# Expert stage: the dots begin once the first head's experts are known, and the searches of heads 1 and 2 stand between them

## The chip, the cores and the metric

One Trainium2 chip, one of its NeuronCores. The metric is the device time of one execution in microseconds (us). Engines are named as in the profile: PE is TensorE, DVE is VectorE, ACT is ScalarE, POOL is GpSimd, SP is the sync engine. 1 MB tiles of weights are issued by SP (DMA queue q1), the gathers of experts by POOL (queue q0). Both queues are served by the same 16 DMA engines.

## The reference, cut to what matters

The program is two blocks on 256 tokens of width 1024. The second block has two layers, and each layer ends in `peer_ffn`, a layer of retrieved experts:

```python
q = (zb @ wq).reshape(128, Hp, 2, half)              # 8 heads, two halves of 128
s = jnp.einsum('thpd,hpnd->thpn', q, subkeys)        # 128 scores a half
s_top, i_top = lax.top_k(s, 16)
cand = s_top[:, :, 0, :, None] + s_top[:, :, 1, None, :]   # 16 x 16 sums
score, flat = lax.top_k(cand.reshape(128, Hp, 256), 16)
expert = i1 * 128 + i2                               # from i_top and flat
gate = jax.nn.softmax(score, axis=-1)
h = jnp.einsum('thkd,td->thk', u_tab[expert], zb)
act = gate * jax.nn.gelu(h, approximate=False)
return jnp.einsum('thk,thkd->td', act, v_tab[expert])
```

Each token has 8 heads of 16 experts, so 128 experts, and each expert is a row of `u` and a row of `v`, 1024 numbers each in float32. With 128 tokens on the partitions, one expert of each token is one gather of 128 rows of 8 KB, 1 MB.

## The kernel before, in words

The expert stage (`*_peer`, once a layer) works through 256 slots: two blocks of 128 tokens (`t`), 8 heads (`h`) in each, 16 experts (`s`) a head. The order of heads is `HEADS`: (0,0), (0,1), ... (0,7), (1,0), ... Each slot passes through five hands:

1. POOL (`pool_peer`, L2828) gathers the slot's 128 rows of `peer_uv` into one of `GB` = 10 row buffers (eight parts of `arena`, then `ada_t` and `silu_cc`). It waits for `experts_ready` at the start of each head (and once more in the middle of the very first), and from the eleventh slot on for `row_free`, that is for the buffer that the slot ten places earlier used.
2. DVE (`dve_peer`, L2856) multiplies the `u` half by the token vector `ztok` and sums it: the dot, into `hbuf`. It waits for the gather (`row_full`).
3. ACT (`act_peer`) takes the dot through GELU (L2727), multiplies by the gate (L2728) and scales the identity by it (`diag`, L2731).
4. PE (`pe_peer`, L2668) adds `diag` times the `v` half into the output banks; its last matmul of the slot increments `row_free`.
5. In the first token block PE also computes the queries of head h+3 (L484) between the slots of head h, for heads 0 to 4. ACT copies them out (L2682, L2691). The weights for them come in the 1 MB tiles of SP.

Which experts a head has is searched by DVE. `dve_first_experts` does it for head 0, in two halves, so that POOL can start with eight slots. `dve_experts` is a generator that does it for any other head. Its `yield`s cut it into 13 pieces: the calls of `next` numbered 1 to 5 are the two top-16 searches, 6 the 256 sums, 7 to 9 the top 16 of the sums, 10 to 13 the expert numbers. Piece 9 ends with `dve_low_score` (L2775), which signals `scores_ready`; piece 13 signals `experts_ready`. It runs in program order with everything else on DVE.

ACT's order matters for the change. Before the slots it does all work of the queries of heads 1 and 2 and then the exponentials of head 0 (L2697). Its loop over heads then begins each head with the exponentials of the *next* head, and only then turns to the 16 slots:

```python
            act_peer_exp(act, step, 0, 0)
            n = l * N_SLOTS
            for i, (t, h) in enumerate(HEADS):
                if i + 1 < len(HEADS):
                    act_peer_exp(act, step, *HEADS[i + 1])
```

`act_peer_exp` starts with a wait for `scores_ready` of its head. DVE in turn waits for `exps_ready` of head i before it normalizes the gates of head i (L2850, L2851) and makes that head's dots.

In the kernel before, DVE runs the whole of `dve_experts` for head 1 ahead of the first dot; behind each dot but the first of a head stands one piece of the search of head i+2.

Of the kernel before, what the change touches and what calls it, by code (L numbers as in the profile page):

```python
# [2 lines left out]

# [35 lines left out]
PEER_H, PEER_K, NKEYS = 8, 16, 128  # L39
# [268 lines left out]
def model_kernel(nc, wstream, adastream, cond, vecs, consts, onehots, tokens, peer_uv, out):  # L308
    ctx = ExitStack()
    with ctx:  # L310
# [126 lines left out]
        class Weights:  # L437
# [5 lines left out]
            def next(self, *key, width=1):  # L443
                while PLAN[self.at] in (None, "+"):
                    self.at += 1
                assert PLAN[self.at] == (*key, width), (PLAN[self.at], key, width)
                tile, b = divmod(self.at, W_TILE)
                if self.tile != tile:
                    self.pe.wait_ge(w_full[tile % W_SLOTS], 16 * (tile // W_SLOTS + 1))
                    if self.tile is not None:  # L450
                        self.owed += 1
                    self.tile = tile
                self.at += 1
                return wt[:, tile % W_SLOTS, b * P:(b + width) * P]
# [2147 lines left out]
        HEADS = [(t, h) for t in range(QT) for h in range(PEER_H)]  # L2602
# [144 lines left out]
        def dve_top16(dve, step, src, vals, idx):  # L2747

            step(dve.max(vals[:, 0:8], src))
            step(dve.max_index(idx[:, 0:8], vals[:, 0:8], src))  # L2750
            yield
            step(dve.match_replace(src, vals[:, 0:8], src, -3.0e38))
            step(dve.max(vals[:, 8:16], src))
            yield
            step(dve.max_index(idx[:, 8:16], vals[:, 8:16], src))

        def dve_experts(dve, step, l, t, h):

            sq = [P, PEER_K, PEER_K]
            for x in range(2):  # L2760
                if t == 0:
                    dve.wait_ge(subs_ready.sem, subs_ready.due(dve))
                yield from dve_top16(dve, step, subs[t][:, h, x * NKEYS:(x + 1) * NKEYS], top_s[:, x, :], top_u[:, x, :])
            yield
            step(dve.tensor_copy(top_i, top_u))
            step(dve.tensor_tensor(cand, top_s[:, 0, :].unsqueeze(2).to_broadcast(sq),
                                   top_s[:, 1, :].unsqueeze(1).to_broadcast(sq), ALU.add))
            yield
            yield from dve_top16(dve, step, cand.rearrange("p a b -> p (a b)"), best[:, h, :], flat_u)
            dve_low_score(dve, step, t, h)  # L2770
            yield
            yield from dve_numbers(dve, step, l, t, h, 0, PEER_K)

        def dve_low_score(dve, step, t, h):
            step(dve.tensor_scalar(low[:, h:h + 1], best[:, h, 0:1], by_token[:, t:t + 1], -1.0, ALU.mult, ALU.mult))  # L2775
            dve.sem_inc(scores_ready.sem, 1)

        def dve_numbers(dve, step, l, t, h, first, n):

            some, sq = slice(first, first + n), [P, n, PEER_K]  # L2780
            dve.tensor_scalar(digit_u[:, 0, some], flat_u[:, some], 4, None, ALU.logical_shift_right)
            step(dve.tensor_scalar(digit_u[:, 1, some], flat_u[:, some], PEER_K - 1, None, ALU.bitwise_and))
            step(dve.tensor_copy(digit[:, :, some], digit_u[:, :, some]))
            for x in range(2):
                yield
                step(dve.tensor_tensor(pick[:, x, some], digit[:, x, some].unsqueeze(2).to_broadcast(sq),
                                       const("iota").unsqueeze(1).to_broadcast(sq), ALU.is_equal))
                step(dve.tensor_tensor(pick[:, x, some], pick[:, x, some], top_i[:, x].unsqueeze(1).to_broadcast(sq),
                                       ALU.mult))
            yield  # L2790
            step(dve.tensor_reduce(digit[:, :, some], pick[:, :, some], AX, ALU.add))
            step(dve.tensor_scalar(digit[:, 0, some], digit[:, 0, some], float(NKEYS), float(l * EXPERTS), ALU.mult,
                                   ALU.add))
            at = h * PEER_K + first
            step(dve.tensor_tensor(experts[:, t, at:at + n], digit[:, 0, some], digit[:, 1, some], ALU.add))
            dve.sem_inc(experts_ready.sem, 1)  # L2796

        def dve_first_experts(dve, step, l):

            sq, half = [P, PEER_K, PEER_K], PEER_K // 2  # L2800
            for x in range(2):
                dve.wait_ge(subs_ready.sem, subs_ready.due(dve))
                for _ in dve_top16(dve, step, subs[0][:, 0, x * NKEYS:(x + 1) * NKEYS], top_s[:, x, :], top_u[:, x, :]):
                    pass
            step(dve.tensor_copy(top_i, top_u))
            step(dve.tensor_tensor(cand, top_s[:, 0, :].unsqueeze(2).to_broadcast(sq),
                                   top_s[:, 1, :].unsqueeze(1).to_broadcast(sq), ALU.add))
            sums = cand.rearrange("p a b -> p (a b)")
            for i, some in enumerate((slice(0, half), slice(half, PEER_K))):
                step(dve.max(best[:, 0, some], sums))  # L2810
                step(dve.max_index(flat_u[:, some], best[:, 0, some], sums))
                if i == 0:
                    for _ in dve_numbers(dve, step, l, 0, 0, 0, half):
                        pass
                    step(dve.match_replace(sums, best[:, 0, some], sums, -3.0e38))
            dve.wait_ge(token_ready.sem, token_ready.due(dve))
            dve_low_score(dve, step, 0, 0)
            for _ in dve_numbers(dve, step, l, 0, 0, half, half):
                pass
# [12 lines left out]
        def dve_peer_out(dve, step, t, done):  # L2832
            dve.wait_ge(row_free, done)
            for half, bank in enumerate(y_banks(t)):
                seg = xT[:, 4 * half:4 * half + 4, t * P:(t + 1) * P]
                step(dve.tensor_tensor(seg, seg, bank.rearrange("p (k t) -> p k t", t=P), ALU.add))
                dve.sem_inc(res_ready.sem, 1)
                part_ready.due(dve)

        def dve_peer(dve, step, l, base):  # L2840
            n = base
            dve_first_experts(dve, step, l)
            for _ in dve_experts(dve, step, l, 0, 1):
                pass
            dve.wait_ge(ztok_ready.sem, ztok_ready.due(dve))
            for i, (t, h) in enumerate(HEADS):
                coming = dve_experts(dve, step, l, *HEADS[i + 2]) if i + 2 < len(HEADS) else iter(())
                g = gates_p[:, t, h * PEER_K:(h + 1) * PEER_K]
                dve.wait_ge(exps_ready.sem, exps_ready.due(dve))
                step(dve.reciprocal(gsum[:, h:h + 1], gsum[:, h:h + 1]))  # L2850
                step(dve.tensor_scalar(g, g, gsum[:, h:h + 1], None, ALU.mult))  # L2851
                dve.sem_inc(gates_ready.sem, 1)
                for s in range(h * PEER_K, (h + 1) * PEER_K):
                    u = rows[n % GB][:, 0:D]
                    dve.wait_ge(row_full[n % GB], 16 * (n // GB + 1))
                    dve.tensor_tensor_reduce(u, u, ztok[:, t], 1.0, 0.0, ALU.mult, ALU.add,  # L2856
                                             hbuf[:, t, s:s + 1]).then_inc(dot_ready.sem, 1)
                    n += 1
                    if s % PEER_K:
                        next(coming, None)  # L2860
                assert next(coming, None) is None
                if (t, h) == (1, 1):
                    dve_peer_out(dve, step, 0, base + SLOTS)
            dve_peer_out(dve, step, 1, base + N_SLOTS)
# [103 lines left out]
        def _(dve):  # L2968
# [27 lines left out]
            for l in range(2):  # L2996
                stages += [
                    lambda l=l: dve_rwkv_in(dve, step, l),
                    lambda l=l: dve_rwkv_core(dve, step, l),
                    lambda l=l: dve_rwkv_out(dve, step, l),  # L3000
                    lambda l=l: dve_nsa_in(dve, step, l),
                    lambda: dve_cmp_swa(dve, step),
                    lambda l=l: dve_rel(dve, step, l),
                    lambda l=l: dve_merge(dve, step, l),
                    lambda l=l: dve_peer(dve, step, l, l * N_SLOTS),
                ]
# [127 lines left out]
```

## Time and profile before

| what | value |
|---|---|
| median of 3 runs (lowest, highest) | 4054.45 us (4051.52, 4054.5) |
| the profiled execution | 4051.08 us |
| its span from first to last instruction | 4049.3 us |
| mean granted TensorE clock | 0.976 |
| PE busy | 3688.2 us, 91% |
| DVE busy | 2606.4 us, 64% |
| ACT busy | 1597.9 us, 39% |
| POOL busy | 691.0 us, 17% |
| gathers issued by POOL | 512, 38.0% of 16 DMA engines' span |

The expert stage of the first layer starts to gather at about 2271 us of the span and makes its last dot at 2942; that of the second layer runs from about 3367 to 4033. The busy shares are averages over stages with different limits, so they say little about these two stretches; those have to be read by themselves.

### The profile page before, as it was taken

What the parts mean: (1) busy time and instruction counts of PE and PEld (TensorE: products, weight loads), DVE (VectorE), ACT (ScalarE), POOL (GpSimd) and SP (SyncE); (2) the same over time, 40 slices, a digit from 0 to 9 for tenths busy, and PEclk for the clock granted to TensorE, in tenths of its full rate; (3) what the DMA queues carried; (4) which work ended last, traced back from release to release, by engine and by line L of the source; (5) the groups of instructions that cost most, each with busy time, mean ns of one, the idle gap of its engine ahead of it and who ended that gap; (6) DMA issues with size and microseconds to landing.
All of it is one profiled execution on the core that took longest, in us unless ns stands there. A gap on an engine that the chain in (4) does not pass through costs nothing. (4 is left out here: it accounts for less than half of the span.)

```text
span 4049.3 us, 65904 instructions
## 1 busy us (share of the span) xinstructions
PE 3688.2 (91%) x25296; PEld 3169.0 (78%) x25296; DVE 2606.4 (64%) x5238; ACT 1597.9 (39%) x3546; POOL 691.0 (17%) x713
## 2 busy tenths in 40 slices
PE   6999989999999998999899998888888999988887
PEld 4888766788788876898778888777777798887776
DVE  6888547677755566656456666777564566677774
ACT  3222537322332245442235444444332354444443
POOL 1000002000000002000000244444300003444442
PEclk9999999999999999999999999999999999999999
DMA  5555211355434420554134699999922257999998
GB/s 226 196 197 182 73 52 53 107 189 178 150 119 137 140 86 12 198 179 155 44 126 157 276 420 420 421 421 420 413 88 73 106 177 318 420 420 420 421 421 333
DMA packets 135065, 905.13 MB, mean 224 GB/s; under 512 B 14855, under 2 KB 15879, under 8 KB 35168
## 3 DMA queue, kind: packets, MB, share of 16 engines
q0 software_dynamic: 95552, 620.97, 38.0%
q1 hardware_dynamic: 39200, 279.96, 19.3%
q8 instruction: 200, 3.28, 0.3%
q14 instruction: 113, 0.93, 0.1%
HBM read 899.79 MB, written 5.28 MB: 224 GB/s over the span
## 5 line engine op out<-in xcount | busy, mean ns | idle before, releaser
L2668 PE MATMUL ps<-arena 128*128 128x128 f32 x6560 | 840.2, 284 | 157.1 <-ACT arena L2731 156.4
L2668 PEld LDWEIGHTS ps<-arena 128*128 128x128 f32 x6560 | 786.8, 196 | 222.8 <-ACT arena L2731 217.7
L2856 DVE CUSTOM_DVE_ANT_0 arena<-arena 128x1024 f32<-128x1024 f32 x410 | 502.2, 1225 | 319.9 <-DMA arena<-peer_uv,arena 318.9
L2828 POOL DMA_INDIRECT arena<-peer_uv,arena x410 | 437.1, 1066 | 1463.9 <-DVEq L2796 858.5
L660 DVE TENSOR_TENSOR w_lo<-wt,w_hi 128x1024 fp32r<-128x1024 f32 x388 | 475.2, 1225 | 313.8 <-ACT w_hi L642 293.7
L642 ACT ACTIVATE w_hi<-wt 128x1024 fp32r<-128x1024 f32 x388 | 409.6, 1061 | 678.1 <-PE ps L695 649.4
L695 PE MATMUL ps<-h_hi,w_hi 128*128 128x512 f32 (+1 forms) x1744 | 642.8, 370 | 13.1 <-ACT h_hi L831 8.4
L695 PE MATMUL ps<-h_hi,w_lo 128*128 128x512 f32 (+1 forms) x1744 | 633.7, 365 | 0.0
L695 PE MATMUL ps<-h_lo,w_hi 128*128 128x512 f32 (+1 forms) x1744 | 594.5, 367 | 10.3 <-DVE h_lo L801 10.0
L484 PE MATMUL ps<-hT,wt 128*128 128x256 f32 (+1 forms) x1696 | 408.7, 379 | 3.8 <-DVE hT L573 3.8
L695 PEld LDWEIGHTS ps<-h_hi,w_hi 128*128 128x128 f32 x1744 | 330.7, 190 | 72.0 <-issue 17.0
L695 PEld LDWEIGHTS ps<-h_lo,w_hi 128*128 128x128 f32 x1744 | 325.3, 190 | 65.9 <-DVE h_lo L801 12.2
L695 PEld LDWEIGHTS ps<-h_hi,w_lo 128*128 128x128 f32 x1744 | 330.5, 190 | 55.0 <-issue 2.1
L2727 ACT ACTIVATE arena<-arena 128x1 f32<-128x1 f32 x512 | 103.3, 202 | 648.0 <-DVE arena L2856 643.6
L484 PEld LDWEIGHTS ps<-hT,wt 128*128 128x128 f32 x1696 | 297.6, 193 | 42.2 <-issue 6.0
L695 PE MATMUL ps<-hid_hi,w_hi 128*128 128x512 f32 (+1 forms) x704 | 255.4, 363 | 0.6 <-DVEq L973 0.6
L695 PE MATMUL ps<-hid_lo,w_hi 128*128 128x512 f32 (+1 forms) x704 | 255.2, 362 | 0.0
L695 PE MATMUL ps<-hid_hi,w_lo 128*128 128x512 f32 (+1 forms) x704 | 255.2, 362 | 0.0
L765 POOL DMA_DIRECT2D ada_t<-adastream x133 | 70.4, 530 | 1079.9 <-DVEq L782 1077.0
L484 PE MATMUL ps<-arena 64*64 64x64 f32 (+5 forms) x3552 | 208.8, 264 | 19.5 <-DVEq L415 9.9
L2731 ACT ACTIVATE arena<-cst,arena 128x128 f32<-128x128 f32 x512 | 205.5, 401 | 27.3 <-PE ps L2668 10.9
L484 PEld LDWEIGHTS ps<-arena 64*64 64x64 f32 (+3 forms) x3552 | 148.8, 146 | 55.4 <-issue 21.2
(342 smaller groups left out, 5277.3 us busy)
## 6 DMA issues: line engine op xcount, KB each, us to landing
wt<-wstream SPq DMA_DIRECT2D x262, 1024.0 KB, 4.8
ada_t<-adastream POOLq DMA_DIRECT2D x133, 512.0 KB, 3.6
arena<-peer_uv,arena POOLq DMA_INDIRECT x410, 20.1
arena<-adastream POOLq DMA_DIRECT2D x11, 512.0 KB, 26.0
bias_by_query<-bias_by_distance POOLq DMA_DIRECT2D x1, 4096.0 KB, 17.7
arena<-bias_by_query POOLq DMA_DIRECT2D x1, 3072.0 KB, 13.1
xT<-tokens SPq DMA_DIRECT2D x1, 2048.0 KB, 14.7
cst<-consts SPq DMA_DIRECT2D x1, 1703.0 KB, 8.5
```

What stands on the lines that cost most here:

```text
L484: ins = pe.matmul(o, lhsT, rhs, start=start, stop=stop, **kw)
L642: self.act.activation(hi, raw_group(g), ACT.Copy).then_inc(w_hi_ready.sem, 1)
L660: self.step(self.dve.tensor_tensor(lo, raw_group(g), hi.bitcast(F32), ALU.subtract))
L695: ins = self.pe.matmul(o, a, b, start=start and i == 0, stop=stop and i == len(pairs) - 1)
L765: pool.dma_start(ada_t[:, i % 2, :], adastream[l * ADA_BLOCKS + m]).then_inc(ada_full[i % 2], 16)
L2668: ins = pe.matmul(y_banks(t)[m // 4][:, (m % 4) * P:(m % 4 + 1) * P], row[:, D + m * P:D + (m + 1) * P], diag[n % DIAGS], start=s == 0 and ...
L2727: step(act.activation(a[:, 0:1], hbuf[:, t, s:s + 1], ACT.Gelu))
L2731: act.activation(diag[n % DIAGS], ident, ACT.Copy, scale=a[:, 1:2]).then_inc(diag_ready.sem, 1)
L2828: pool.indirect_dma_start(out=rows[n % GB], out_offset=None, in_=peer_uv, in_offset=bass.IndirectOffsetOnAxis(ap=experts[:, t, s:s + 1], a ...
L2856: dve.tensor_tensor_reduce(u, u, ztok[:, t], 1.0, 0.0, ALU.mult, ALU.add, hbuf[:, t, s:s + 1]).then_inc(dot_ready.sem, 1)
```

## The change

`dve_experts` of head 1 is no longer run as a whole ahead of the dots. It is chained in front of that of head 2, and both stand between the 16 dots of head 0: behind each dot, the first too, two pieces are taken. All other heads are as before, one piece a dot.

```diff
@@ def dve_peer(dve, step, l, base):
             n = base
             dve_first_experts(dve, step, l)
-            for _ in dve_experts(dve, step, l, 0, 1):
-                pass
             dve.wait_ge(ztok_ready.sem, ztok_ready.due(dve))
             for i, (t, h) in enumerate(HEADS):
-                coming = dve_experts(dve, step, l, *HEADS[i + 2]) if i + 2 < len(HEADS) else iter(())
+                ahead = HEADS[1:3] if i == 0 else HEADS[i + 2:i + 3]
+                coming = itertools.chain.from_iterable(dve_experts(dve, step, l, *head) for head in ahead)
...
-                    if s % PEER_K:
+                    for _ in range(len(ahead) if s % PEER_K or i == 0 else 0):
                         next(coming, None)
                 assert next(coming, None) is None
```

No instruction is added or removed on any engine; some of DVE's change places. ACT's, PE's, POOL's and SP's orders are untouched. The generator of head 1 ends within its 13th `next`, and the chain goes on in that same call with the first piece of head 2, so the two searches take 25 calls.

## Rows read from the trace of the kernel before

**Rows 1.** The page, part 2: GB/s in 40 equal slices of the span.
```profile
GB/s 226 196 197 182 73 52 53 107 189 178 150 119 137 140 86 12 198 179 155 44 126 157 276 420 420 421 421 420 413 88 73 106 177 318 420 420 420 421 421 333
```

**Rows 2.** Busy time by stretch of the first expert stage (us, engines, clock, DMA).
```profile
core 0: us, PE busy (x) PEld busy (x) DVE busy (x) ACT busy (x) POOL busy (x), PEclk, DMA share, GB/s
2290.00:2310.00 20.00, 15.59 (x113) 15.28 (x114) 17.27 (x45) 8.54 (x28) 6.68 (x6) 0.83 1.02 422
...
2910.00:2930.00 20.00, 15.56 (x123) 14.04 (x123) 9.98 (x17) 7.18 (x24) 4.68 (x5) 1.00 1.01 421
```

**Rows 3.** Timeline of POOL: start, length, what, idle before it and releaser.
```profile
2270.97 1.05 POOL L2828 DMA_INDIRECT arena<-peer_uv,arena  x1 [414.15 <-DVEq L2796]
...
2282.40 0.97 POOL L2828 DMA_INDIRECT silu_cc<-peer_uv,arena  x1 [0.30 <-issue]
2298.43 1.54 POOL L2828 DMA_INDIRECT arena<-peer_uv,arena  x1 [15.06 <-PE ps L2668]
2300.64 1.19 POOL L2828 DMA_INDIRECT arena<-peer_uv,arena  x1 [0.68 <-PE ps L2668]
...
2332.14 1.37 POOL L2828 DMA_INDIRECT arena<-peer_uv,arena  x1 [1.12 <-PE ps L2668]
2338.49 0.94 POOL L2828 DMA_INDIRECT arena<-peer_uv,arena  x1 [4.98 <-PE ps L2668]
...
3394.22 1.65 POOL L2828 DMA_INDIRECT arena<-peer_uv,arena  x1 [15.32 <-PE ps L2668]
```

**Rows 4.** Timeline of DVE from the search of head 1 on.
```profile
2275.21 0.29 DVE L2749 MAX8 arena<-xT 128x8 f32<-128x128 f32 x1 [0.37 <-ACTq L2693]
...
2280.04 0.29 DVE L2749 MAX8 arena<-xT 128x8 f32<-128x128 f32 x1 [3.03 <-ACTq L2693]
...
2285.10 0.21 DVE L2775 TENSOR_SCALAR arena<-arena,small 128x1 f32<-128x1 f32 x1
...
2288.73 0.18 DVE L2795 TENSOR_TENSOR arena<-arena 128x16 uint32<-128x16 f32 x1
2290.16 0.16 DVE L2850 RECIPROCAL arena<-arena 128x1 f32<-128x1 f32 x1 [1.26 <-ACTq L2699]
...
2290.78 1.23 DVE L2856 CUSTOM_DVE_ANT_0 arena<-arena 128x1024 f32<-128x1024 f32 x1 [0.19 <-DVE arena L2851]
...
2291.93 1.22 DVE L2856 CUSTOM_DVE_ANT_0 arena<-arena 128x1024 f32<-128x1024 f32 x1
...
2309.22 1.23 DVE L2856 CUSTOM_DVE_ANT_0 silu_cc<-silu_cc,arena 128x1024 f32<-128x1024 f32 x1 [0.39 <-DMA silu_cc<-peer_uv,arena]
```

**Rows 5.** Timeline of ACT: exponentials of heads 0 and 1, then the first slot.
```profile
2289.52 0.40 ACT L2697 ACTIVATE arena<-arena,small 128x16 f32<-128x16 f32 x1 [0.19 <-ACT hT L2691]
2289.83 0.19 ACT L2697 ACTIVATION_READ_ACCUMULATOR arena<-arena,small 128x1 f32 x1
...
2290.44 0.19 ACT L2697 ACTIVATION_READ_ACCUMULATOR arena<-arena,small 128x1 f32 x1
2292.10 1.28 ACT L2727 ACT_TABLE_LOAD   x1 [1.48 <-DVE arena L2856]
```

**Rows 6.** Timeline of PE: its first slot of the stage.
```profile
2294.41 3.74 PE L2668 MATMUL ps<-arena 128*128 128x128 f32 x16 [5.36 <-ACT arena L2731]
```

**Rows 7.** DMA queues from 2270 to 2307: packets, MB, share.
```profile
q0 software_dynamic: 1438, 10.51, 68.2%
q1 hardware_dynamic: 576, 4.19, 27.9%
```

**Rows 8.** DMA queues from 2268 to 2275.3: no packet of q0.
```profile
q1 hardware_dynamic: 180, 1.34, 48.5%
```

**Rows 9.** DMA queues in the next microsecond, from 2275.3 to 2276.3.
```profile
q0 software_dynamic: 11, 0.09, 21.3%
```

**Rows 10.** The weight tile issued between 2270.0 and 2270.5, and q1's first packets (2271.3 to 2271.6).
```profile
wt<-wstream SPq DMA_DIRECT2D x1, 1024.0 KB, 5.2
...
q1 hardware_dynamic: 5, 0.04, 116.2%
```

More of the change, by code:

```diff
@@ L1 @@
+import itertools
 import math
```

## The prediction

> **What bounds the kernel now.** I read the page's slices first, because the busy shares say nothing of one stage. In both expert stages the rate stands at some 420 GB/s, slice after slice, and well below that everywhere else [rows 1]. The table of stretches of the first stage shows it closer: 1.01 to 1.02 of the DMA engines' time, 418 to 422 GB/s in every 20 us stretch between 2290 and 2930, 32 of them, of which the first and the last are shown; PE and DVE both have stretches of under 16 us in 20 [rows 2]. So the stage is a fixed amount of transfer at a fixed rate: 256 gathers of 1.05 MB and a few weight tiles. One MB tile takes 1.05 MB / 421 GB/s = 2.49 us. A faster or better ordered DVE can't shorten this. What can move the end is an idle stretch of the DMA engines, and such a stretch is lost for good, since nothing later has slack to make it up.
>
> The second thing to read is how the stage starts. POOL issues ten gathers from 2270.97 to 2282.40, fills all ten buffers, and then stands for 15.06 us until PE has finished the first slot; the eleventh gather goes out at 2298.43, and the next 2.21 us later [rows 3]. In this pause the DMA engines live on what is queued. That is the cover to be watched: how long it lasts, and when the first buffer is freed with the change.
>
> **The supply of the DMA engines.** Up to 2307 they moved 10.51 MB for q0 and 4.19 MB for q1, four weight tiles [rows 7]. Ten gathers are 10.49 MB, so in the mean over the engines the ten gathers are through at 2306.9. Some engines are later: the dot of the tenth row started at 2309.22 after waiting 0.39 us for its data, so the last of its bytes were reported by then [rows 4]. The engines' own work of the ten gathers thus ends between 2306.9 and 2309.2, and I take the middle, 2308.05. Before the change the eleventh gather comes 8.5 us ahead of the earlier bound, and nothing shows.
>
> **The change part by part.**
>
> *The search of head 1 before the dots goes.* It stands from 2275.21 to 2288.91, and 3.03 us of it are a wait. But DVE then still waits 1.26 us for ACT, and the reciprocal starts at 2290.16 [rows 4]. ACT gives the exponentials of head 0 only after the queries of heads 1 and 2: its L2697 starts at 2289.52 [rows 5]. So removing the search lets no dot start earlier: DVE idles from about 2275 to 2290.16, and the first dot stays at 2290.78. The search was free where it stood. Gain: 0.
>
> *The search of head 1 now stands between the dots.* Each dot takes 1.15 us (2290.78 to 2291.93), and pieces 1 to 9 of head 1 take 2285.31 - 2275.21 - 3.03 = 7.07 us [rows 4]. Two pieces stand behind each dot, so piece 9 is behind the fifth dot. Its scores are known at 2290.78 + 5 x 1.15 + 7.07 = 2303.6. The data of rows 0 to 4 are there by then, as they were for the same dots before; no wait for DMA comes in.
>
> *What is queued behind those scores.* ACT asks for the exponentials of head 1 before the first GELU of head 0. Before, both sets ran in one go, from 2289.52 to 2290.63, 0.50 us each with its accumulator read (2289.83 + 0.19 - 2289.52), and the load of the GELU table began at 2292.10, released by the first dot [rows 5]. Now ACT stands until 2303.6 + 0.15 (the step from ACT's accumulator read, over at 2290.02, to DVE's reciprocal at 2290.16 [rows 4, 5]), takes 0.50 for the exponentials, and starts the table load at 2304.35. From that load to PE's first matmul of a slot it is 2294.41 - 2292.10 = 2.31 us [rows 5, 6]. PE starts at 2306.7 in place of 2294.41, 12.25 us later. Behind PE stand `row_free` and POOL: the first slot takes 4.02 us until POOL moves (2294.41 to 2298.43), at PE's lower clock in both kernels: it stood idle for 5.36 us before this slot, and its granted clock is 0.83 in the mean of that stretch [rows 2, 6]. The eleventh gather goes out at 2298.43 + 12.25 = 2310.7 [rows 3].
>
> *The hole in the transfers.* The queue ran dry at 2308.05 (2306.9 to 2309.2), the gather is issued at 2310.7, and its first bytes move a latency L later. For L the trace has one row of the same instruction: issued at 2270.97, no packet of q0 before 2275.3, some in the microsecond after, so L = 4.3 [rows 3, 8, 9]. It might be shorter on idle engines, because q1 was at work just then; the lower bound is SP's own issue, which shows first packets about 1.2 us after it [rows 10]. I take 4.3, the row of the same instruction. The hole is 2310.7 + 4.3 - 2308.05 = 7.0 us, with ends 2310.7 + 1.2 - 2309.2 = 2.7 and 2310.7 + 4.3 - 2306.9 = 8.1.
>
> The Trainium skill ("DMA: Bandwidth & Descriptors", Specifications) gives about 1 us for the first byte of a gather issued by GpSimd; by it the hole would be some 3.7 us, a rival below. The same page (SWDGE vs HWDGE vs iDMA) says that a DMA engine takes turns between its queues; by that rule a gather that was ready sooner would have shared the engines with q1 sooner, which speaks for the 4.3 us of the trace.
>
> *After the hole.* POOL now gets buffers at PE's pace, 2.21 us a slot, and the engines need 2.49, so the queue fills again, but slowly. The hardest test is the start of head 1: ACT loads its two tables there and PE stands, so one step of POOL is 6.35 us in place of 2.21 [rows 3]. Shifted by 12.25, the sixteenth gather after the hole is issued at 2344.4 and the seventeenth at 2350.7, with first bytes at 2355.0. The engines are then busy until 2315.0 + 16 x 2.49 + 2.49 (one weight tile) = 2357.3. It holds with 2.3 us to spare. I add nothing. The weight tile comes later too, because PE frees its slot, but it stays one tile.
>
> *The rest costs nothing.* The 25 calls end behind the thirteenth dot; the search of head 1 is done at 2290.78 + 7 x 1.15 + 10.7 = 2309.5 (the 10.7 is the whole search without its wait), and POOL wants its numbers for the seventeenth gather, at 2324. Head 2's scores are wanted by ACT only after 16 slots. DVE's piece of head 3 will wait up to 3 us for ACT, with PE ten slots behind; the dots catch up at some 2 us against 2.49. SP's queue has nothing moved.
>
> *The sum.* The second stage has the same program and the same start (its POOL stands for 15.32 us where the first stands for 15.06 [rows 3]), so each layer loses 7.0 us, together 14.0. The profiled execution took 4051.08 us, which makes 4065.1. The median of the runs is 3.4 us above that execution and their lowest is at its level, so I set half of that on top: 4067.
>
> **The rivals.**
>
> *The cover nearly holds.* L is near 1.2 and the last engine is at work until 2309.2: 2.7 us a layer, 5.4 in all, 4058.5. By 3.7 a layer it is 7.4, 4060. Both are within 0.2% (8.1 us), which is about what a measurement of this kernel tells from no change. For it: the 4.3 us were seen with q1 busy. It decides below a hole of 4.05 us. Against: it needs both ends at once, or L under 1.5. This is also the case that the change does next to nothing.
>
> *The delay is exposed in full.* If the refilled queue is too shallow (the 2.3 us to spare at head 1 are used up by PE's low clock over a second slot, or by uneven engines), the whole 12.25 us of PE's delay come through, 24.5 in all, 4077. For it: little is left to spare. Against: the pace of 2.21 against 2.49, and a delay longer than its cover can't cost more than itself.
>
> *Faster.* The DMA engines don't set the end, and DVE does: then the dots gain from the 10.7 us of search taken out ahead of them, in the best case 1.4 us before the wait for ACT, so 2.8 in all and within 0.2%. To exceed it, the exponentials of head 0 would have to be ready at 2275, not at 2290 [rows 5]; then all of the dots start 13 us sooner and up to 26 us in all could be won, 4028. ACT's order excludes it.
>
> **How the numbers follow.** The forecast (a hole of 4.05 to 9 us a layer) has 0.74, the cover that nearly holds 0.13, the full delay 0.11, faster 0.02. The forecast's own range is 4062 to 4072; the range given reaches to 4060.5 below and 4074 above, which leaves out a part of both neighbours. Faster by over 0.2% is 0.02, within 0.2% is 0.13, slower 0.85.
>
> **What would show it.** First dot at about 2290.8, as before, with DVE idle for some 15 us ahead of it. ACT's second L2697 at 2303.8, PE's first slot near 2306.7, the eleventh gather near 2310.7, in the second stage the same 12.25 us later than before. DMA share well under 1 for 7 us around 2308 to 2315, then 1.01 again, also at head 1. The last dot of each stage later by the sum of the holes. I am wrong if dots begin sooner, if ACT makes a GELU before the exponentials of head 1, or if the DMA share shows no hole or several.

## The result: 0.41% slower, and the profile after

| what | before | changed |
|---|---|---|
| median of the compared runs (lowest, highest; runs) | 4054.43 us (4051.52, 4057.66; 6) | 4070.88 us (4067.96, 4073.42; 6) |
| ratio to before, 95% interval | | 1.0041 (1.0031 to 1.0051) |
| the profiled execution | 4051.08 us | 4067.96 us |
| its span, granted clock | 4049.3 us, 0.976 | 4066.2 us, 0.974 |
| first gather to last dot, first stage | 670.74 us | 678.52 us |
| first gather to last dot, second stage | 664.99 us | 674.46 us |

The change costs 16.45 us in the medians and 16.88 us between the two profiled executions; the two expert stages alone lost 7.78 and 9.47 us, together 17.25. Nothing else has to be explained. In the changed file the lines of POOL, ACT and PE stand one further down (the gather is L2829, the exponentials L2698, PE's slot L2669).

POOL in the changed kernel: start, length, what, idle before it and releaser.

```profile
2271.42 1.05 POOL L2829 DMA_INDIRECT arena<-peer_uv,arena  x1 [414.20 <-DVEq L2797]
...
2282.85 0.94 POOL L2829 DMA_INDIRECT silu_cc<-peer_uv,arena  x1 [0.30 <-issue]
2312.86 0.93 POOL L2829 DMA_INDIRECT arena<-peer_uv,arena  x1 [29.07 <-PE ps L2669]
2315.08 0.94 POOL L2829 DMA_INDIRECT arena<-peer_uv,arena  x1 [1.29 <-PE ps L2669]
...
2346.58 1.20 POOL L2829 DMA_INDIRECT arena<-peer_uv,arena  x1 [1.28 <-PE ps L2669]
2353.06 1.58 POOL L2829 DMA_INDIRECT arena<-peer_uv,arena  x1 [5.27 <-PE ps L2669]
...
3416.77 0.93 POOL L2829 DMA_INDIRECT arena<-peer_uv,arena  x1 [30.49 <-PE ps L2669]
```

POOL's pause is 29.07 us where it was 15.06 [rows 3]. I measure all kernels below by G, the time from the first gather to the eleventh: 27.46 us before in either stage, now 41.44 (2312.86 - 2271.42) and 42.61. What PE waited for stands in the rows of DVE, ACT and PE, in this order, changed kernel:

```profile
2292.51 0.16 DVE L2850 RECIPROCAL arena<-arena 128x1 f32<-128x1 f32 x1 [17.22 <-ACTq L2700]
```

```profile
2292.17 0.19 ACT L2698 ACTIVATION_READ_ACCUMULATOR arena<-arena,small 128x1 f32 x1
2306.02 0.40 ACT L2698 ACTIVATE arena<-arena,small 128x16 f32<-128x16 f32 x1 [13.66 <-DVEq L2777]
...
2306.68 1.28 ACT L2728 ACT_TABLE_LOAD   x1 [0.16 <-ACT arena L2698]
```

```profile
2308.98 3.60 PE L2669 MATMUL ps<-arena 128*128 128x128 f32 x16 [17.59 <-ACT arena L2732]
```

Read backwards: PE waits 17.59 us for ACT's `diag`. ACT stands 13.66 us ahead of its second exponentials, released by DVE's low score, and only behind them loads the GELU table. DVE stood 17.22 us before its first dot, waiting for ACT (the same row of before has 1.26 [rows 4]). The loop from ACT to DVE and back costs what the prediction says it costs. The transfers in the table of stretches, changed kernel (us, five engines, clock, DMA share, GB/s):

```profile
2304.00:2306.00 2.00, 0.00 (x0) 0.00 (x0) 1.86 (x6) 0.00 (x0) 0.00 (x0) 0.50 1.01 422
2306.00:2308.00 2.00, 0.00 (x0) 0.00 (x0) 1.86 (x6) 1.81 (x4) 0.00 (x0) 0.50 0.65 270
2308.00:2310.00 2.00, 1.02 (x5) 1.02 (x5) 1.86 (x5) 1.84 (x8) 0.00 (x0) 0.50 0.01 4
2310.00:2312.00 2.00, 2.00 (x11) 2.00 (x11) 1.79 (x6) 0.99 (x4) 0.00 (x0) 0.50 0.00 0
2312.00:2314.00 2.00, 2.00 (x17) 1.95 (x17) 1.86 (x7) 0.79 (x3) 0.93 (x1) 0.93 0.00 0
2314.00:2316.00 2.00, 2.00 (x19) 1.95 (x18) 1.90 (x9) 0.79 (x3) 0.92 (x1) 1.00 0.71 164
2316.00:2318.00 2.00, 2.00 (x19) 1.95 (x18) 1.90 (x7) 0.79 (x3) 0.72 (x2) 1.00 1.04 434
2318.00:2320.00 2.00, 2.00 (x19) 1.95 (x18) 1.93 (x5) 0.62 (x3) 0.89 (x2) 1.00 0.95 369
2320.00:2322.00 2.00, 2.00 (x19) 1.95 (x18) 1.86 (x7) 0.57 (x2) 0.89 (x2) 1.00 0.98 324
2322.00:2324.00 2.00, 2.00 (x19) 1.95 (x18) 1.82 (x7) 0.00 (x0) 0.71 (x2) 1.00 0.98 344
...
2350.00:2370.00 20.00, 20.00 (x153) 19.52 (x152) 16.85 (x43) 7.52 (x28) 8.78 (x8) 0.92 1.02 422
```

At 2304 the engines are full; from about 2307.3 they move next to nothing; the first packet after that is seen at 2314.47, 1.6 us behind the gather of 2312.86. Then come some microseconds at a share near 1 but only 324 to 369 GB/s, and then 420 again. At head 1 (the last row) there is no second hole. To put one number on it I sum, in 3 us stretches from 4 to 139 us after the first gather, what falls short of 420.5 GB/s, as time: 8.7 and 10.2 us in the two stages, against stages longer by 7.8 and 9.5. I call this the deficit. Before it is -0.1 in both.

### The profile page after: what moved, and what is told of

Its sections match the earlier page's. It is cut to its first block and busy times, and to the rows that moved or that the text cites. A ratio compares the mean times of both kernels' runs of the same rounds, so it can differ in the third digit from the quotient of the medians.

```text
span 4066.2 us, 65906 instructions
## 1 busy us (share of the span) xinstructions
PE 3676.5 (90%) x25296; PEld 3167.8 (78%) x25296; DVE 2606.6 (64%) x5238; ACT 1591.4 (39%) x3546; POOL 691.8 (17%) x713
## 5 line engine op out<-in xcount | busy, mean ns | idle before, releaser
L2669 PE MATMUL ps<-arena 128*128 128x128 f32 x6560 | 839.8, 284 | 178.6 <-ACT arena L2732 178.0
L2669 PEld LDWEIGHTS ps<-arena 128*128 128x128 f32 x6560 | 792.3, 196 | 234.4 <-ACT arena L2732 227.2
L2829 POOL DMA_INDIRECT arena<-peer_uv,arena x410 | 441.7, 1077 | 1480.0 <-DVEq L2797 857.7
L696 PE MATMUL ps<-h_hi,w_hi 128*128 128x512 f32 (+1 forms) x1744 | 642.4, 370 | 13.1 <-ACT h_hi L832 8.4
```

The costliest lines, as they stand in the source:

```text
L696: ins = self.pe.matmul(o, a, b, start=start and i == 0, stop=stop and i == len(pairs) - 1)
L2669: ins = pe.matmul(y_banks(t)[m // 4][:, (m % 4) * P:(m % 4 + 1) * P], row[:, D + m * P:D + (m + 1) * P], diag[n % DIAGS], start=s == 0 and ...
L2829: pool.indirect_dma_start(out=rows[n % GB], out_offset=None, in_=peer_uv, in_offset=bass.IndirectOffsetOnAxis(ap=experts[:, t, s:s + 1], a ...
```

## The experiments

All with their G, deficit and loss of the stage (first gather to last dot, against before), first and second stage. "First dot" is counted from the first gather; before it is 19.81 and 19.92. The last column is explained under the fifth group; "none" stands where it would be negative.

| kernel | us, ratio (95%) | first dot | G | deficit | stage loss | G - 32.7 |
|---|---|---|---|---|---|---|
| changed | 4070.88, 1.0041 (1.0031 to 1.0051) | 21.71, 22.42 | 41.44, 42.61 | 8.7, 10.2 | 7.8, 9.5 | 8.7, 9.9 |
| r_again | 4073.72, 1.0047 (1.0033 to 1.0061) | 22.52, 22.53 | 42.44, 42.74 | 10.3, 10.4 | 9.6, 9.8 | 9.7, 10.0 |
| r_explate | 4053.42, 0.9997 (0.9988 to 1.0007) | 22.61, 24.25 | 30.29, 32.21 | -0.2, 2.3 | 0.1, 2.2 | none |
| r_hold5 | 4065.57, 1.0026 (1.0016 to 1.0036) | 22.59, 26.31 | 37.41, 41.07 | 5.4, 9.0 | 4.9, 8.2 | 4.7, 8.4 |
| r_hold8 | 4077.16, 1.0056 (1.0042 to 1.0070) | 22.63, 26.38 | 42.67, 46.43 | 10.7, 13.8 | 9.8, 13.1 | 10.0, 13.7 |
| r_scores | 4052.70, 1.0000 (0.9991 to 1.0009) | 19.81, 19.91 | 27.49, 27.58 | -0.1, -0.1 | 0.0, -0.2 | none |
| r_early | 4052.89, 1.0001 (0.9992 to 1.0010) | 9.94, 9.39 | 24.58, 25.34 | -0.1, -0.1 | 0.0, -0.3 | none |
| r_tile_first | 4067.00, 1.0033 (1.0020 to 1.0045) | 19.80, 19.91 | 39.72, 40.10 | 7.3, 7.3 | 6.6, 6.9 | 7.0, 7.4 |

### 1. The changed kernel again, a later place for ACT's exponentials, and ACT held ahead of its first GELU

`r_again` is the changed kernel unedited. `r_explate` leaves DVE's new order as it is and lets ACT ask for the exponentials of head 1 only behind the twelfth slot of head 0:

```diff
             for i, (t, h) in enumerate(HEADS):
-                if i + 1 < len(HEADS):
+                if 0 < i < len(HEADS) - 1:
                     act_peer_exp(act, step, *HEADS[i + 1])
...
+                    if i == 0 and s == 11:
+                        act_peer_exp(act, step, *HEADS[1])
```

`r_hold5` and `r_hold8` do the opposite: the kernel before, with DVE's old order. ACT makes the exponentials of heads 0 and 1 in one go as before, and is then held ahead of its first GELU until 5 or 8 dots are made (`r_hold8` has `+ 8`):

```diff
                 act.wait_ge(gates_ready.sem, gates_ready.due(act))
+                if i == 0:
+                    act.wait_ge(dot_ready.sem, l * N_SLOTS + 5)
                 for s in range(h * PEER_K, (h + 1) * PEER_K):
```

> The changed kernel once more, unedited. Theory A (ACT's wait for the scores of head 1 frees the first buffer some 12 us later, the DMA engines run dry, and the hole is the loss): again 12 to 19 us slower, with no packets for about 7 us. In the changed kernel's trace the first dot also came 1.9 us (first stage) and 2.9 us (second) later after the first gather than in the kernel before. If that belongs to the change it is there again in both stages; if it is chance, it differs and the time moves with it.

> The changed kernel, with ACT's exponentials of head 1 moved behind the twelfth slot of head 0. DVE keeps the changed order. Theory A: the hole is gone, the eleventh gather goes out about 27.5 us after the first one as in the kernel before, and the time is that of the kernel before within 3 us. Theory B (DVE is the cause: 26 pieces between 16 dots keep it full for 40 us and the dots come late): still 12 to 17 us slower, since DVE's order is that of the changed kernel.

> The kernel before with one wait added: in each layer ACT starts the first GELU when five dots are made. DVE's order is that of the kernel before. That is about 7.1 us later than before, inside the cover of 8.5 to 10 us that the queued gathers give. Theory A: no change, within 3 us. Theory B: no change. A theory that any delay of ACT and PE is paid in full: 14 us slower.

> The same with eight dots: ACT starts about 12.6 us later than in the kernel before, as in the changed kernel, while DVE keeps the order of the kernel before. Theory A: the hole opens, some 5.4 us without packets plus 1 to 2 us of slow refill in each stage, 11 to 16 us slower in all. Theory B: no change, since the searches stand where they stood.

POOL and ACT in `r_explate`:

```profile
2274.13 1.05 POOL L2831 DMA_INDIRECT arena<-peer_uv,arena  x1 [414.52 <-DVEq L2799]
...
2304.42 0.94 POOL L2831 DMA_INDIRECT arena<-peer_uv,arena  x1 [17.90 <-PE ps L2669]
```

```profile
2295.78 0.19 ACT L2698 ACTIVATION_READ_ACCUMULATOR arena<-arena,small 128x1 f32 x1
...
2298.06 1.28 ACT L2728 ACT_TABLE_LOAD   x1 [2.09 <-DVE arena L2858]
```

The table load now follows the first dot, and the whole loss is gone though DVE makes every search piece where the changed kernel makes it. ACT's place is the cause; that DVE's longer work between dots sets the end is refuted. `r_hold8` shows the converse, POOL first:

```profile
2315.09 0.94 POOL L2830 DMA_INDIRECT arena<-peer_uv,arena  x1 [30.31 <-PE ps L2668]
```

```profile
2308.72 1.28 ACT L2729 ACT_TABLE_LOAD   x1 [13.84 <-DVE arena L2858]
```

With the search and the exponentials of head 1 done ahead of the dots, as before, ACT's late table load gives a pause of 30.31 us, and the kernel takes 23.6 us more (4077.16 against 4053.57), more than the change and more than the 11 to 16 us that I expected; a first dot up to 6.5 us late adds to it. I had put `r_hold5` inside the cover, at no loss; it cost 12.0 us (4065.57). Two things failed in that expectation. First, the cover is shorter than I had it: with the first dot on time G would be some 34.6 us (an estimate, 37.41 less the 2.78 us that the dot was late), 7.2 us over that of before, and only 5.2 us are free (group 5). Second, in all four kernels the first dot is later than before, by 2.7 to 2.8 us in the first stage and 2.6 to 6.5 us in the second, and everything behind it with it. (`r_explate` has a small deficit in its second stage, 2.3 us at the start of head 1, with G = 32.2 just under the limit; its median doesn't show it.) That the late start isn't tied to one order of DVE shows in `r_hold5` and `r_hold8`, which have the old one.

### 2. Only the part of the search that ACT wants

`r_scores`, on the kernel before: nine pieces of head 1, up to its low score, ahead of the dots; the other four and head 2 between them, two pieces a dot.

```diff
             dve_first_experts(dve, step, l)
-            for _ in dve_experts(dve, step, l, 0, 1):
-                pass
+            second = dve_experts(dve, step, l, *HEADS[1])
+            for _ in range(9):
+                next(second)
             dve.wait_ge(ztok_ready.sem, ztok_ready.due(dve))
...
+                coming = itertools.chain.from_iterable(second if head == HEADS[1] else dve_experts(dve, step, l, *head)
+                                                       for head in ahead)
```

> The changed kernel, but pieces 1 to 9 of head 1 (up to its scores) run before the first dot; its numbers and the whole search of head 2 stand between the dots, two pieces a dot. Theory A: the time of the kernel before within 3 us, for only the scores are on the way to the first GELU, and DVE stood idle when those nine pieces run. Theory B predicts a loss of some 10 us, since 16 calls still stand between the dots.

Table of stretches, `r_scores`:

```profile
2290.00:2310.00 20.00, 14.05 (x95) 13.01 (x94) 15.26 (x44) 7.69 (x23) 5.23 (x4) 0.83 1.01 422
2310.00:2330.00 20.00, 18.77 (x146) 16.96 (x145) 16.87 (x40) 10.05 (x35) 8.46 (x8) 1.00 1.01 421
```

No hole and no difference: G is 27.49 as before. So of the search only the nine pieces ahead of `scores_ready` have a price between the dots. Moving the rest is free, and gives nothing.

### 3. Dots that really begin early

`r_early`, on `r_explate`: ACT makes the exponentials of head 0 ahead of its work for the queries of heads 1 and 2, directly behind its signal `ztok_ready`.

```diff
                     act.sem_inc(ztok_ready.sem, 1)
+                    act_peer_exp(act, step, 0, 0)
-            act_peer_exp(act, step, 0, 0)
             n = l * N_SLOTS
```

> The changed kernel, with the exponentials of head 0 moved ahead of the queries of heads 1 and 2 on ACT, and those of head 1 behind the twelfth slot. The dots can now begin when the first row has landed, at about 2281 in place of 2290.8, and PE's first slot follows its own queries at about 2289 in place of 2294.4. Theory A: the DMA engines set the end, so the time is that of the kernel before within 3 us although dots and first slot are earlier. A theory in which an earlier first dot is worth its time: 10 to 20 us faster.

DVE in `r_early`:

```profile
2279.13 0.16 DVE L2852 RECIPROCAL arena<-arena 128x1 f32<-128x1 f32 x1 [0.22 <-DVE arena L2798]
...
2284.98 1.23 DVE L2858 CUSTOM_DVE_ANT_0 arena<-arena 128x1024 f32<-128x1024 f32 x1 [5.42 <-DMA arena<-peer_uv,arena]
2289.76 1.23 DVE L2858 CUSTOM_DVE_ANT_0 arena<-arena 128x1024 f32<-128x1024 f32 x1 [2.23 <-DMA arena<-peer_uv,arena]
```

The first dot comes 9.9 us earlier, now held by its own data, and the time stays (1.0001, against 10 to 20 us faster if an earlier first dot were worth its time). This is what the bound predicts: a stage of fixed transfers doesn't end sooner for earlier dots.

### 4. Nine row buffers

Both kernels with one row buffer less (`silu_cc`, the last of the list, dropped):

```diff
+        rows.pop()
         GB = len(rows)
```

> The kernel before with nine row buffers in place of ten. The queued gathers end 2.5 us sooner, the first freed buffer comes when it did. Theory A: the cover (8.5 to 10 us) shrinks to 6 to 7.5 us and still holds: no change, within 3 us.

> The changed kernel with nine row buffers. Theory A: each hole grows by one gather, 2.5 us, so 5 us over the changed kernel, about 21 us slower than the kernel before. If the loss had nothing to do with how long the queued gathers last, it would stay at 16.

`r_before9` took 4053.33 us, 1.0001 (0.9992 to 1.0010), deficit -0.1: one tile less of supply, 2.49 us, is still covered, so before has more than that to spare. `r_after9` took 4071.56 us, 1.0044 (1.0030 to 1.0058), deficits 9.5 and 9.8. Its table of stretches:

```profile
2305.00:2308.00 3.00, 0.00 (x0) 0.00 (x0) 2.75 (x9) 0.92 (x3) 0.00 (x0) 0.50 0.85 355
2308.00:2311.00 3.00, 1.11 (x5) 1.11 (x6) 2.86 (x7) 2.83 (x9) 0.00 (x0) 0.50 0.01 3
2311.00:2314.00 3.00, 3.00 (x15) 2.91 (x15) 2.68 (x11) 1.12 (x5) 0.06 (x1) 0.50 0.00 0
2314.00:2317.00 3.00, 3.00 (x21) 2.86 (x20) 2.83 (x11) 0.79 (x4) 0.94 (x2) 0.81 0.48 109
```

The hole opens 33.3 us after the first gather (2274.23) where ten buffers last 35.9. By the sum a tile less should have cost some 2.5 us a layer on top of the change. It cost 2.2 us more in all (18.7 against 16.5), because in this kernel the first dot was on time (19.80 and 19.91): its first gather with a freed buffer, its tenth, came 39.7 and 40.1 us after the first, so PE's delay was smaller by about what the tile was worth. The 32.7 of the table's last column is for ten buffers; with nine it would be 30.2, which gives 9.5 and 9.9 here; the stages lost 8.5 and 9.1.

### 5. What the cover is

In the kernels with a hole and ten buffers the stage's loss is G - 32.7 us to within 1 us (last column; 5.1 and 5.1 for `r_eight` below, whose stages lost 5.1 and 5.5). The 32.7 is my reading of these runs, not a row; it comes to 35.9 us of supply, less 1.6 us from issue to first packet, less some 1.6 us lost in the slow refill. With G = 27.46 before, 5.2 us of delay are free, and each further one costs itself.

Where the first dot's lateness comes from was the next question. PE between its queries and ACT's copy of one, changed kernel:

```profile
2279.37 3.62 PE L485 MATMUL ps<-hT,wt 128*128 128x256 f32 x16
2285.49 0.71 PE L485 MATMUL ps<-wt,arena 128*128 128x128 f32 x4 [2.50 <-issue]
```

```profile
2284.94 0.38 ACT L2683 ACTIVATE arena<-ps 128x256 f32<-128x256 f32 x1 [4.69 <-remote]
```

PE loses 2.50 us once here, where it elsewhere loses 0.59 between queries. The matmul of 2285.49 reads a weight tile (`wt`) and the query that ACT copies for it. ACT starts that copy at 2284.94, after 4.69 us in place of 2.78, although PE's row of the query ends at 2282.99. The almost 2 us between are in no row; `remote` says that the profile names no releaser on this core. A late tile isn't shown here: in the program PE turns to these weights' tile in the middle of the query ahead, and the two tiles issued with the first gathers moved as before. Queue q1 from 1 us ahead of the first gather to 9 us behind it, before and changed:

```profile
q1 hardware_dynamic: 288, 2.10, 53.3%
q1 hardware_dynamic: 288, 2.10, 57.6%
```

The lateness goes with the profiled execution rather than with the program. PE's queries are late in the profiles of the changed kernel, its repeat, `r_explate`, `r_hold5`, `r_hold8` and the three `r_eight` kernels below. The same eight profiles, and no others, give no time from issue to landing for the tiles; before and changed, part 6 of the page:

```profile
wt<-wstream SPq DMA_DIRECT2D x262, 1024.0 KB, 4.8
wt<-wstream SPq DMA_DIRECT2D x262, 1024.0 KB
```

And `r_after9` is on time, though its first nine gathers and everything ahead of them are those of the changed kernel. What makes an execution late isn't known.

What tiles and gathers do to each other shows in a kernel that starts its gathers earlier. `r_eight` (on before) finds the first 8 experts from the 8 best of each half and a table of 8 x 8 sums, and the other 8 afterwards; `r_eight_early` is this on `r_early`, `r_eight_after` on the changed kernel.

```diff
-                for _ in dve_top16(dve, step, subs[0][:, 0, x * NKEYS:(x + 1) * NKEYS], top_s[:, x, :], top_u[:, x, :]):
-                    pass
+                step(dve.max(top_s[:, x, 0:half], src[x]))
+                step(dve.max_index(top_u[:, x, 0:half], top_s[:, x, 0:half], src[x]))
...
+            few, few_sq = sums[:, 0:half * half], [P, half, half]
...
+            step(dve.max(best[:, 0, 0:half], few))
+            step(dve.max_index(flat_u[:, 0:half], best[:, 0, 0:half], few))
+            for _ in dve_numbers(dve, step, l, 0, 0, 0, half, half):
+                pass
```

> The kernel before with the first eight experts of head 0 found from the top 8 of each half and an 8 x 8 table of sums (the eight best sums can only lie there), the rest of head 0 afterwards. The first gather goes out some 3.3 us sooner after the scores. Theory A: without a hole the stage's length from the first gather is fixed at about 671 and 665 us, so this is worth its time: some 6 us faster in all than the kernel before. PE's first slot doesn't move, so the eleventh gather comes 30.8 us after the first one in place of 27.5, still under the 32.7 that the runs so far give as the limit.

> The same search of head 0 in the kernel with the exponentials of head 0 early and those of head 1 behind the twelfth slot. The eleventh gather comes about 28 us after the first, with more room than in the kernel with only the shorter search. Theory A: again some 6 us faster than the kernel before, and no idle stretch in the transfers.

> The same search of head 0 in the changed kernel. Theory A: the first gather is 3.3 us earlier, but the hole opens 3.3 us earlier too and ends when it did, since its end hangs on ACT and PE. So the time is that of the changed kernel, 14 to 19 us slower than the kernel before. A theory in which every stage is shorter by what its first gather gains: 6 us faster than the changed kernel.

| kernel | us, ratio (95%) | first dot | G | deficit | stage loss |
|---|---|---|---|---|---|
| r_eight | 4057.99, 1.0013 (1.0004 to 1.0022) | 30.42, 30.16 | 37.80, 37.84 | 4.4, 5.2 | 5.1, 5.5 |
| r_eight_early | 4052.43, 0.9996 (0.9987 to 1.0005) | 7.49, 7.67 | 35.86, 39.50 | 2.4, 5.8 | 3.1, 6.7 |
| r_eight_after | 4082.04, 1.0070 (1.0056 to 1.0084) | 30.07, 28.38 | 50.00, 48.60 | 16.6, 15.3 | 16.9, 15.5 |

PE and POOL in `r_eight`:

```profile
2281.94 2.68 PE L484 MATMUL ps<-hT,wt 128*128 128x256 f32 x6 [3.73 <-DMA wt<-wstream]
...
2286.22 5.02 PE L484 MATMUL ps<-hT,wt 128*128 128x256 f32 x16
```

```profile
2269.05 1.05 POOL L2838 DMA_INDIRECT arena<-peer_uv,arena  x1 [411.19 <-DVEq L2796]
...
2306.85 1.81 POOL L2838 DMA_INDIRECT arena<-peer_uv,arena  x1 [25.54 <-PE ps L2668]
```

Here SP issues the tile at 2271.61, 2.56 us behind the first gather; before, it went out 0.49 us ahead of it. In the first 5 us behind its issue q1 moves 0.27 MB, where it moved 1.43 MB before. PE waits 3.73 us for this tile, and behind the wait its matmuls run at a granted clock of 0.50 (the 1.2 GHz level): sixteen take 5.02 us in place of 3.62. The first dot is at 2299.47, 8.7 us later than before and not earlier, and the buffers run out before the first is freed. I had expected some 6 us less and G = 30.8; G is 37.80, and the kernel takes 3.8 us more. How much of the late dot belongs to the earlier gathers and how much to the kind of execution described above can't be told apart from one profile; the tile's slow start and PE's wait for it are in the rows.

`r_eight_early` was expected to gain the same 6 us without a hole. Its first dot is early, but PE's own queries are late in it too, so G is 35.86 and 39.50, over the limit, and the time is that of the kernel before (the interval includes 1). `r_eight_after` takes 27.9 us more, where I had expected 14 to 19. The rule of the 32.7 us was found before these three kernels ran, and it gives their stage losses within 0.5 us (5.1, 5.1; 3.2, 6.8; 17.3, 15.9).

`r_tile_first`, on the changed kernel, keeps most gathers out of the tile's way: POOL holds its third gather until the weight tile that PE's queries of heads 1 and 2 share has landed.

```diff
+                if (t, s) == (0, 2):
+                    tile = PLAN.index(("peer_subkeys", base // N_SLOTS, 0, 3 * P, 1)) // W_TILE
+                    pool.wait_ge(w_full[tile % W_SLOTS], 16 * (tile // W_SLOTS + 1))
```

> The changed kernel, with one wait added on POOL: the third gather of each layer goes out when the weight tile that the queries of heads 1 and 2 need has landed. In the runs so far the first dot came 19.8 to 26.4 us after the first gather, without a change of its code, and the hole grew by as much. If that lateness comes from tiles and gathers sharing the engines in the first microseconds, the first dot is back at about 20 us after the first gather in both stages, the holes shrink to about 7 us of lost transfer each, and the kernel is some 14 us slower than the kernel before. If the lateness has another cause, it varies as before, 2 to 3 us or more over 19.8.

POOL, PE and DVE in `r_tile_first`:

```profile
2272.71 1.05 POOL L2832 DMA_INDIRECT arena<-peer_uv,arena  x1 [414.72 <-DVEq L2797]
2274.07 0.97 POOL L2832 DMA_INDIRECT arena<-peer_uv,arena  x1 [0.30 <-issue]
2277.66 0.94 POOL L2832 DMA_INDIRECT arena<-peer_uv,arena  x1 [2.63 <-DMA wt<-wstream]
...
2312.43 0.94 POOL L2832 DMA_INDIRECT arena<-peer_uv,arena  x1 [25.11 <-PE ps L2669]
```

```profile
2284.87 0.71 PE L485 MATMUL ps<-wt,arena 128*128 128x128 f32 x4 [0.59 <-ACTq L2685]
```

```profile
2291.89 0.16 DVE L2853 RECIPROCAL arena<-arena 128x1 f32<-128x1 f32 x1 [15.45 <-ACTq L2700]
```

PE's 2.50 us are 0.59, the first dot is at 19.80 and 19.91 us, both stages have the same deficit (7.3), and the kernel takes 12.55 us more than before where the changed one takes 16.45 and its repeat 20.15. (The hold also puts eight gathers off by 2.3 us, with the engines busy meanwhile.) So with the first dot on time the moved search costs 12.55 us, predicted 14.0. The changed kernel and its repeat take 3.9 and 7.6 us more than this; their stages lost 3.7 and 5.9 us more, with the first dot late. `r_after9`, also on time, agrees: its stages lost 17.6 us, and without the two tiles of 2.49 us it is 12.6. What `r_tile_first` doesn't show is that the hold made the dot punctual. PE's queries are on time without a hold in `r_scores`, `r_early`, `r_before9` and `r_after9` as well.

## Why the prediction was right, and where its sum was off

- **The bound.** Right. Every kernel without a hole has the stage's length of before within 0.3 us, with the dots 10 us earlier too (`r_early`), and in every other the loss of a stage is the transfers' deficit within 1 us.
- **The search before the dots was free.** Right: DVE now waits 17.22 us for ACT. But "the first dot stays at 2290.78" failed: it came 1.9 and 2.5 us later, counted from the first gather. No step of the prediction has this; it took PE's queries, which ACT and DVE wait for, as ending when they ended before.
- **ACT's exponentials of head 1 behind the search.** Right, and shown from both sides (`r_explate`, `r_hold8`). From first dot to ACT's exponentials it is 2306.02 - 2293.13 = 12.9 us, predicted 2303.8 - 2290.78 = 13.0; table load to PE 2.30, predicted 2.31; PE's first slot to POOL 3.88, predicted 4.02, with the granted clock at 0.50 in these rows, the 1.2 GHz level.
- **The eleventh gather.** Predicted at G = 39.7; `r_tile_first`, where the first dot is on time, has 39.72 and 40.10. The changed kernel has 41.44 and 42.61, by the late first dot.
- **The hole.** 7.0 us a layer was predicted for G = 39.7, and `r_tile_first` has deficits of 7.3. But its terms were mis-sized and nearly cancel, so that the size came out so well is luck. The latency L was put at 4.3 us; on idle engines it is 1.6 (2312.86 to 2314.47; 3416.77 to 3418.4), near the lower bound of 1.2. Against that the supply ended at 35.9 us after the first gather, the earlier of the two bounds, and not at 37.1, and the refill, which I added at nothing, costs about 1.6 us through its low rate.
- **Head 1 after the hole.** Right: no second hole; its gather is at 2353.06, predicted 2350.7, later by the late first dot.
- **The total.** 4067 predicted, 4070.88 measured, inside the forecast's own range of 4062 to 4072; the repeat, 4073.72, is above it. The missing 3.9 us are mostly the late first dot: the two stages lost 17.25 us where the sum has 14.0, and G is 1.7 and 2.9 us above the predicted 39.7.

The Trainium skill ("DMA: Bandwidth & Descriptors", Specifications) gives about 1 us to the first byte of a gather issued by GpSimd; the trace has 1.6 us on idle engines, nearer to it than the 4.3 us that I took, but a hole sized by it alone would have left out the refill. The same page (SWDGE vs HWDGE vs iDMA) says that an engine takes turns between its queues. The trace of `r_eight` agrees: with gathers ahead of it the tile moves 0.27 MB in its first 5 us, where it moved 1.43 MB before, while the gathers move 1.52.

Of the rivals, the cover that nearly holds had L right and still fell, since the supply ended early. The full delay exposed fell too: G grew by 14.0 and 15.1 us, the stages by 7.8 and 9.5. Faster fell as argued: ACT's order kept the dots back, and even without it (`r_early`) nothing is won.

Open is why PE's queries, and with them the first dot, are late in some profiles and not in others. SP issues the tile 0.49 us ahead of the first gather before and 0.50 in the changed kernel, q1 moves the same bytes in both, and yet PE loses 2.50 us in one and none in the other. It isn't the moved search: `r_hold5` and `r_hold8` have the old order and are late, `r_scores`, `r_after9` and `r_tile_first` have the new one and are on time. Since every late profile and no punctual one lacks the landing times of the tiles, a difference between single executions is the likeliest, and no run here tests it; that gathers and tiles share the engines is shown only for `r_eight`.

## What to carry to other kernels

In a stage bound by transfers, follow each moved step to the instruction that frees the next buffer, and price it as the longest time the queue stays without a new transfer, less the cover, which is queued work minus issue latency and refill. Work that gives another engine its input has a different price from the rest of the same routine: nine pieces of this search cost 7 us a layer between the dots, the last four nothing. Check the loss by summing the transfers' shortfall; if it equals the stage's growth, nothing else is left to find.

## What the runs showed of the hardware that I had not expected

- A gather's first packet comes 1.6 us after its issue on idle engines; with weight tiles queued it was 4.3 us [rows 3, 8, 9]. In `r_eight`, whose first gather has no tile ahead of it, it is 1.7 us (issue at 2269.05, no packet of q0 up to 2270.75, 12 packets in the 0.3 us behind that).
- After the engines ran dry they show a share of 0.95 to 0.98 at only 324 to 369 GB/s for about 6 us, at 2318 to 2324 (420 is the usual), while gathers come one at a time.
- With gathers queued ahead of it, a tile of the other queue moved 0.27 MB in its first 5 us in place of 1.43, PE waited 3.73 us for it and then ran at a granted clock of 0.50; `r_eight`, whose gathers start sooner, took 3.8 us more.
